# Order of the decay levels and of the constants' loads in a gMLP/HGRN2 trunk kernel

## What is computed

```python
h = _rmsnorm(x, mix_norm[l])
z = h @ w_in[l]
u, v, q, f, i, og, gates = _split_cols(z, IN_SIZES)
a = _gmlp_branch(gelu(u), gelu(v), gm_ln_g[l], gm_ln_b[l], gm_ws[l], gm_bs[l])
b = _hgrn2_branch(q, f, i, og, lower_bounds[l], hg_norm_g[l])
y = sigmoid(gate_a) * (a @ w_br_gm[l]) + sigmoid(gate_b) * (b @ w_br_hg[l])
x = x + y @ w_out[l]
x = x + _conv_ffn(_rmsnorm(x, ffn_norm[l]), w_up[l], conv_w[l], conv_b[l], w_down[l])
# then a last rmsnorm.  Inside _gmlp_branch: w masked to blocks of 64 positions,
mixed = einsum('hij,bnjhd->bnihd', w, layernorm(v)) + bs
# Inside _hgrn2_branch, per head and chunk, G the running sum of log(forget):
A = einsum('bhid,bhijd,bhjd->bhij', q, exp(G_i - G_j) where causal, k)
o = A @ v + (q * exp(G)) @ state
state = exp(G_last) * state + (k * exp(G_last - G))^T @ v
```

## Time and profile before

| | us |
|---|---|
| median of 3 runs (lowest to highest) | 2891.79 (2891.43 to 2895.05) |
| the profiled execution | 2889.99 |
| its span, first to last instruction | 2888.2 |
| around the span | 1.8 |
| TensorE busy | 2858.6 |
| VectorE, ScalarE, GpSimd busy | 1511.7, 724.3, 196.2 |
| mean granted TensorE clock | 0.997 |

### The profile page before, as it was taken

The page is one execution under the profiler, slowest core; times in us unless marked ns, Lnnn a source line. Parts: engine busy times, 40 slices in busy tenths (PEclk is TensorE's granted clock), DMA queues, the critical chain, the costliest instruction groups (busy, mean ns, idle before and its releaser), DMA issues.

```text
span 2888.2 us, 33313 instructions
## 1 busy us (share of the span) xinstructions
PE 2858.6 (99%) x13264; PEld 2380.4 (82%) x13264; DVE 1511.7 (52%) x2879; ACT 724.3 (25%) x986; POOL 196.2 (7%) x87
## 2 busy tenths in 40 slices
PE   8999999999999999999999999999999999999998
PEld 6888888888888888888888888888888888888886
DVE  6876677756266335553335634555333653455521
ACT  5332244434212112221112211222112220122200
POOL 3333410015000000000000000000000000000000
PEclk9999999999999999999999999999999999999999
DMA  8657988889744465556563446555666345555554
GB/s 299 233 187 236 318 288 289 292 303 330 256 146 147 164 227 191 190 194 231 213 222 132 161 170 219 194 189 192 234 216 218 132 146 190 208 198 191 190 211 167
DMA packets 121977, 614.58 MB, mean 213 GB/s; under 512 B 13536, under 2 KB 13792, under 8 KB 74080
## 3 DMA queue, kind: packets, MB, share of 16 engines
q1 hardware_dynamic: 121824, 612.46, 60.2%
HBM read 474.00 MB, written 138.41 MB: 212 GB/s over the span
## 4 chain that ended last, share of the span: by engine, by line
PE 94%; DVE 2%; DMA 1%; issue 1%; POOL 1%; ACT 0%; POOLq 0%; SPq 0%; DVEq 0%; ACTq 0%
PE bank L1008 27%; PE bank L1009 27%; PE bank L1013 27%; PE bank L1075 3%; PE bank L1062 2%; PE bank L1063 2%; PE bank L1064 2%; DMA raw<-w_units 1%; POOL w_both L409 1%; PE bank L1148 1%; PE bank L1177 0%; DMA w_split<-w_both 0%; PE bank L1169 0%; PE bank L1022 0%; PE bank L1019 0%
## 5 line engine op out<-in xcount | busy, mean ns | idle before, releaser
L1008 PE MATMUL bank<-h_hi,w_both 128*128 128x512 f32 x2400 | 944.4, 393 | 0.0
L1009 PE MATMUL bank<-h_lo,w_both 128*128 128x512 f32 x2400 | 934.2, 389 | 0.0
L1013 PE MATMUL bank<-h_hi,w_both 128*128 128x512 f32 x2400 | 593.4, 389 | 0.0
L1008 PEld LDWEIGHTS bank<-h_hi,w_both 128*128 128x128 f32 x2400 | 450.7, 188 | 96.4 <-issue 3.8
L1009 PEld LDWEIGHTS bank<-h_lo,w_both 128*128 128x128 f32 x2400 | 450.6, 188 | 96.1 <-issue 3.8
L1013 PEld LDWEIGHTS bank<-h_hi,w_both 128*128 128x128 f32 x2400 | 450.5, 188 | 93.5
L926 DVE TENSOR_TENSOR z<-bank,rms_inv 128x512 f32<-128x512 f32 x176 | 121.8, 692 | 337.8 <-PE bank L1013 337.4
L1009 PE MATMUL bank<-g_lo,w_both 128*128 128x512 f32 x704 | 273.9, 389 | 0.0
L1008 PE MATMUL bank<-g_hi,w_both 128*128 128x512 f32 x704 | 273.9, 389 | 0.0
L939 DVE SCALAR_TENSOR_TENSOR conv<-z,params,conv 128x512 f32<-128x512 f32 x352 | 263.5, 750 | 7.0 <-DVE halo L929 0.8
L409 POOL TENSOR_TENSOR w_both<-raw,w_both 128x1024 fp32r<-128x1024 f32 x80 | 195.0, 2438 | 533.3 <-ACT w_both L423 493.3
(11 more groups left out here) (220 smaller groups left out, 3139.3 us busy)
## 6 DMA issues: line engine op xcount, KB each, us to landing
w_both<-w_split SPq DMA_DIRECT2D x372, 1024.0 KB, 4.8
w_split<-w_both SPq DMA_DIRECT2D x248, 512.0 KB, 5.6
raw<-w_units SPq DMA_DIRECT2D x124, 512.0 KB, 5.3
x_in<-x_t SPq DMA_DIRECT2D x32, 256.0 KB, 5.4
res<-x_t SPq DMA_DIRECT2D x32, 256.0 KB, 5.1
out<-res SPq DMA_DIRECT2D x32, 256.0 KB, 6.9
masks<-masks_in SPq DMA_DIRECT2D x1, 1152.0 KB, 9.7
gm_w<-gm_wt SPq DMA_DIRECT2D x1, 256.0 KB, 6.3
```

Of the source, the lines that this page charges most:

```text
L1008: pe.matmul(dst, w_hi[slot][:, off + k, :], rhs_hi(k), start=first and k == 0, stop=False)
L1009: pe.matmul(dst, w_hi[slot][:, off + k, :], rhs_lo(k), start=False, stop=False)
L1013: mm = pe.matmul(dst, w_lo[slot][:, off + k, :], rhs_hi(k), start=False, stop=last and k == n - 1)
```

## The change

On SP the three constants are issued behind units 2, 3 and 4 of tile 0, and the masks behind unit 5. GpSimd's part of `gm_w` moves to its turn for unit 8. TensorE's product of `lnb_row` and `gm_w` moves from behind unit 1 to behind unit 7 and from bank 6 to bank 3; TensorE no longer waits for VectorE's addition of `bs_row`, which moves behind the statistics of v in tile 0, and so does the wait for the masks.

In each of the 16 heads VectorE makes keys and totals of all levels first, then the queries of all levels, each still from `qp` of the level before; `og_act` stands between the copy and the product of level 16. TensorE's `flip` waits for the last copied keys; the levels run from 2 up to 64, each behind a wait for its own `qr`; the masked copies follow the same order.

```diff
-    names = ["forget", "floor", "qp1"]
+    names = ["forget", "floor", "qp1", "qr1"]
     for s in LEVELS:
-        names += [f"qr{s}", f"qp{2 * s}", f"kl{2 * s}", f"kr{2 * s}", f"t{2 * s}"]
+        names += [f"kl{2 * s}", f"kr{2 * s}", f"t{2 * s}"]
+    for s in LEVELS:
+        names += ([f"qr{s}"] if s > 1 else []) + [f"qp{2 * s}"]
...
-        for a, b in ((gm_w[:, :, :], gm_wt), (lnb_row[:, :], ln_b.broadcast_to([P, NH * P])),
-                     (bs_row[:, :], gm_bs.broadcast_to([P, NH * P]))):
-            sp.dma_start(a, b).then_inc(consts_in, 16)
-        sp.dma_start(masks[:, :], masks_in).then_inc(masks_here, 16)
...
                 if t == 0:
                     first_tile(u)
+                    if 2 <= u < 5:
+                        sp.dma_start(consts[u - 2][0], consts[u - 2][1]).then_inc(consts_in, 16)
+                    if u == 5:
+                        sp.dma_start(masks[:, :], masks_in).then_inc(masks_here, 16)
...
-            if u == 2:
+            if u == 8:
                 po.wait_ge(consts_in, N_CONST)
-                po.wait_ge(lo_made, 2)
+                po.wait_ge(lo_made, 8)
                 po.memset(gm_w[GM_CHUNK:P, :, 0:GM_CHUNK], 0.0).then_inc(pro_pool, 1)
...
         dve.wait_ge(ident_here, 16)
-        dve.wait_ge(consts_in, N_CONST)
-        dve.wait_ge(pro_pe, 1)
-        dve.tensor_tensor(gm_b[:, :, :], blocks(bank[6][:, :], P), blocks(bs_row[:, :], P), ALU.add).then_inc(pro_dve, 1)
         norm_inv(0)
...
+            if t == 0:
+                dve.wait_ge(consts_in, N_CONST)
+                dve.wait_ge(pro_pe, 1)
+                dve.tensor_tensor(gm_b[:, :, :], blocks(bank[3][:, :], P), blocks(bs_row[:, :], P),
+                                  ALU.add).then_inc(pro_dve, 1)
+                dve.wait_ge(masks_here, 16)
+                dve.wait_ge(pro_dve, 8)
...
+                    dve.tensor_tensor(k2_l, k_l, spread(t_r, s), ALU.mult).then_inc(*head_dve.did(f"kl{2 * s}"))
+                    dve.tensor_copy(k2_r, k_r).then_inc(*head_dve.did(f"kr{2 * s}"))
+                    dve.tensor_tensor(total[2 * s][:, :], t_l, t_r, ALU.mult).then_inc(*head_dve.did(f"t{2 * s}"))
+                for s in LEVELS:
...
+                    then(f"qp{s}")
+                    dve.tensor_copy(blocks(q_right[s][:, :], s), q_r).then_inc(*head_dve.did(f"qr{s}"))
+                    if s == 16:
+                        dve.wait_ge(*head_act.at("sig_og", it))
+                        dve.tensor_tensor(og_act[:, :], sig_og[:, :], bank[1][:, :], ALU.mult).then_inc(evac[1], 1)
+                    then(f"qr{s}")
+                    dve.tensor_tensor(q_r, blocks(q_right[s][:, :], s), spread(t_l, s),
+                                      ALU.mult).then_inc(*head_dve.did(f"qp{2 * s}"))
...
-                pe.wait_ge(*head_dve.at(f"t{P}", it))
+                pe.wait_ge(*head_dve.at(f"kr{P}", it))
                 flip(bank[2], kp[P]).then_inc(*head_pe.did("k_tok"))
-                for a, b in ((64, 32), (16, 8), (4, 2)):
+                for a, b in ((2, 4), (8, 16), (32, 64)):
+                    pe.wait_ge(*head_dve.at(f"qr{a}", it))
                     level(a)
+                    pe.wait_ge(*head_dve.at(f"qr{b}", it))
                     level(b).then_inc(*head_pe.did(f"s{a}_{b}"))
                 from_h(t, U_HEAD + 5, u, 1, used + 2)
-                pe.wait_ge(*head_dve.at("m2", it))
+                pe.wait_ge(*head_dve.at("m64", it))
```

More of the change, by code:

```diff
@@ L239, in build @@
     head_act = Steps(sem("head_act"), ["i_head", "sig_f", "sig_q", "sig_og", "k_tok", "o_sq", "o_rms"])
-    head_pe = Steps(sem("head_pe"), ["s1", "k_tok", "s64_32", "s16_8", "s4_2", "update", "o", "mix", "o_sum"])
-    names = ["forget", "floor", "qp1"]
+    head_pe = Steps(sem("head_pe"), ["s1", "k_tok", "s2_4", "s8_16", "s32_64", "update", "o", "mix", "o_sum"])
+    names = ["forget", "floor", "qp1", "qr1"]
     for s in LEVELS:
-        names += [f"qr{s}", f"qp{2 * s}", f"kl{2 * s}", f"kr{2 * s}", f"t{2 * s}"]
+        names += [f"kl{2 * s}", f"kr{2 * s}", f"t{2 * s}"]
+    for s in LEVELS:
+        names += ([f"qr{s}"] if s > 1 else []) + [f"qp{2 * s}"]
     head_dve = Steps(sem("head_dve"), ["k"] + names + [f"vh{c}" for c in range(NC)]
-                     + ["m1", "m0", "m64", "m32", "m16", "m8", "m4", "m2", "st0", "st1", "st2", "st3", "st4",
+                     + ["m1", "m0", "m2", "m4", "m8", "m16", "m32", "m64", "st0", "st1", "st2", "st3", "st4",
                         "mix", "a", "a_hi", "a_lo", "inv", "unit", "b", "b_hi", "b_lo"])
@@ L361, in _ @@
         sp.dma_start(ident[:, :], ident_in).then_inc(ident_here, 16)
-        for a, b in ((gm_w[:, :, :], gm_wt), (lnb_row[:, :], ln_b.broadcast_to([P, NH * P])),
-                     (bs_row[:, :], gm_bs.broadcast_to([P, NH * P]))):
-            sp.dma_start(a, b).then_inc(consts_in, 16)
-        sp.dma_start(masks[:, :], masks_in).then_inc(masks_here, 16)
+        consts = ((gm_w[:, :, :], gm_wt), (lnb_row[:, :], ln_b.broadcast_to([P, NH * P])),
+                  (bs_row[:, :], gm_bs.broadcast_to([P, NH * P])))
         for t in range(NT):
@@ L716, in _ @@
         dve.wait_ge(pro_pool, 2)
-        dve.wait_ge(masks_here, 16)
-        dve.wait_ge(pro_dve, 8)
+        dve.wait_ge(pro_dve, 7)
         def final_out(turn):
@@ L774, in _ @@
                                   ALU.mult).then_inc(*head_dve.did("qp1"))
+                then("qp1")
+                q_r = halves(qp[:, :], 1)[1]
+                dve.tensor_copy(q_right1.unsqueeze(3), q_r.rearrange("p (n q) s -> p n q s", n=NC)).then_inc(*head_dve.did("qr1"))
                 for s in LEVELS:
-                    then(f"t{s}" if s > 1 else "qp1")
-                    q_l, q_r = halves(qp[:, :], s)
+                    if s > 1:
+                        then(f"t{s}")
                     k_l, k_r = halves(kp[s][:, :], s)
                     k2_l, k2_r = halves(kp[2 * s][:, :], s)
-                    t_l, t_r = halves(total[s][:, :], 1)
-                    t_l, t_r = t_l[:, :, 0], t_r[:, :, 0]
+                    t_l, t_r = (v[:, :, 0] for v in halves(total[s][:, :], 1))
+                    dve.tensor_tensor(k2_l, k_l, spread(t_r, s), ALU.mult).then_inc(*head_dve.did(f"kl{2 * s}"))
+                    dve.tensor_copy(k2_r, k_r).then_inc(*head_dve.did(f"kr{2 * s}"))
+                    dve.tensor_tensor(total[2 * s][:, :], t_l, t_r, ALU.mult).then_inc(*head_dve.did(f"t{2 * s}"))
+                for s in LEVELS:
+                    q_r = halves(qp[:, :], s)[1]
+                    t_l = halves(total[s][:, :], 1)[0][:, :, 0]
                     if s == 1:
-                        dve.tensor_copy(q_right1.unsqueeze(3), q_r.rearrange("p (n q) s -> p n q s", n=NC)).then_inc(*head_dve.did("qr1"))
                         then("qr1")
@@ L786, in _ @@
                                           t_l.rearrange("p (n q) -> p n q", n=NC), ALU.mult).then_inc(*head_dve.did("qp2"))
[L787 to L796, removed]
+                        continue
+                    then(f"qp{s}")
[6 more added lines that the diff above has]
+                                      ALU.mult).then_inc(*head_dve.did(f"qp{2 * s}"))
                 dve.wait_ge(*ln_dve.at("inv", t))
@@ L802, in _ @@
                                       spreads[:, 1, c:c + 1], ALU.subtract, ALU.mult).then_inc(*head_dve.did(f"vh{c}"))
-                for n, (s, made, before) in enumerate(((1, "s1", f"t{P}"), (0, "s1", "m1"), (64, "s64_32", "m0"),
-                                                       (32, "s64_32", "m64"), (16, "s16_8", "m32"),
-                                                       (8, "s16_8", "m16"), (4, "s4_2", "m8"), (2, "s4_2", "m4"))):
+                for n, (s, made, before) in enumerate(((1, "s1", f"vh{NC - 1}"), (0, "s1", "m1"), (2, "s2_4", "m0"),
+                                                       (4, "s2_4", "m2"), (8, "s8_16", "m4"), (16, "s8_16", "m8"),
+                                                       (32, "s32_64", "m16"), (64, "s32_64", "m32"))):
                     dve.wait_ge(*zero_dve.at("scores", t))
@@ L1109, in _ @@
                     for_first_tokens(n, [bank[b] for b in I_BANKS], True)
[L1110 to L1115, removed]
                     if n == 2:
@@ L1124, in _ @@
                     sums_spread(bank[5], r_hi, r_lo, done_dve.at("sum_lo", t - 1), fin_pe)
-            pe.wait_ge(pro_dve, 8)
             if t:
@@ L1133, in _ @@
             if t == 0:
+                pe.wait_ge(pro_pool, 3)
+                for h in range(NH):
+                    mm = pe.matmul(bank[3][:, h * P:(h + 1) * P], lnb_row[:, h * P:(h + 1) * P], gm_w[:, h, :],
+                                   start=True, stop=True)
+                mm.then_inc(pro_pe, 1)
                 pe.wait_ge(*norm_act.at(f"hi{KD - 1}", 0))
```

## The result

| | before | changed |
|---|---|---|
| median, lowest to highest, us | 2894.88, 2891.43 to 2896.08 (5 runs) | 2878.29, 2877.56 to 2878.95 (5 runs) |
| the profiled execution | 2889.99 | 2877.56 |
| its span | 2888.2 | 2875.8 |

The ratio is 0.9946, 95% interval 0.9935 to 0.9956: 0.54% faster. The forecast was 2881.5; the measured median lies 0.7 us under the low end of the range, 2879.0.

A forecast was written before the change was run, and what follows sets the result against it. TensorE, busy 99% of the span, was taken as the bound, leaving idle or low-clock time to win. Start 5.5 plus tile 0's heads 4.8 make 10.3 us: 2891.8 - 10.3 = 2881.5, range 2879.0 to 2886.5.

The forecast's parts named there:

- The start, net 5.5: Tile 0's start: raw 2 lands sooner without constants and masks ahead, unit 4 starts 6.4 us sooner; 5.5 us won net.
- the 0.9 given back: Behind unit 7: the gm_w matmuls taken out of the start run there instead, costing 0.9 us.
- The full-pipe reading at 400 GB/s: Loads at the start: transfers fill the pipe, no latency; 1.97 MB removed ahead of raw 2 saves 4.9 us.
- The heads in tile 0, net 4.8: Tile 0's four heads: the flip's wait goes, less 0.05 us of new wait a head; 4.8 us won net.
- the wait of 1.24 goes, four times: 4.96: TensorE's flip in tile 0's heads: last keys are ready before TensorE comes, saving 4.96 us.
- The upper bound of 5.0: Tile 0's heads: the most the forecast thought could be won there, 5.0 us.
- `qr64` and the last masked copy: Tile 0's heads, what is late next: level 64's queries by 0.7 us in time, the last masked copy a tie.
- Tiles 1 to 3, "nothing won": The 12 heads of tiles 1 to 3: extra 0.7 us on VectorE lies inside 5 us of slack; no gain or loss.
- A: Start: the clock falls all the same, costing 1.7 us and 0 to 1 more of wait; chance 0.12.
- D: Every head: short matmul groups step with VectorE, the clock falls 16 times, 27.2 us, giving 2908.7; chance 0.02.
- B: Tile 0's heads: last masked copy late; 2890.5 us if one more GpSimd run intervenes; chance 0.08 for over a us a head.
- C: Units 3 to 8: moved constants return 4.9 us as late raw or low parts, giving 2886.4; chance 0.05.

The follow-up runs named there:

- masks_front: The changed kernel with the 1152 KB of masks issued at the start again, only the three small constants moved: median 2882.65 us, ratio 0.9962.
- heads: The kernel before with only the change's new order of work in the heads, constants as before: median 2884.5 us, ratio 0.9969.
- flip_qr32: The changed kernel with TensorE's flip waiting for the copied queries of level 32 instead of the last keys: median 2882.77 us, ratio 0.9963.
- flip_qp64: The changed kernel with the flip waiting for qp64, the query product of level 32: median 2887.42 us over 12 runs, ratio 0.9982.
- late_mask: The changed kernel with VectorE's v_head made twice in each head, ahead of the masked copies: median 2884.75 us, ratio 0.9967.
- order: The kernel before with only TensorE's levels and the masked copies reordered, from 2 up to 64: median 2894.3 us, ratio 1.0003.
- consts: The kernel before with only the moves of constants, masks, memset, gm_w matmuls and bs_row addition, heads as before: median 2885.94 us, ratio 0.9980.
- squares: The changed kernel with ScalarE's squares of x 4 and 5 ahead of unit 2's high part in tile 0: median 2877.53 us, ratio 0.9943.
- again: The kernel before, unchanged, run again as a control: median 2894.9 us, ratio 1.0005.
- flip_late: The changed kernel with the flip waiting for the last product of the queries: median 2920.1 us, ratio 1.0090.

## Why the prediction was right, and where it was not

- *The start, net 5.5: right, a little small.* The moved part alone gives 5.2 us on the lowest times and 6.6 on the medians; in its profile the spread comes 6.4 us sooner, and with the 0.9 given back that is the 5.5 of the sum. By its steps, in the changed kernel: landing at 16.2 (15.9 measured), last sum near 26.5 (26.1), a wait of 0.3 (0.7), unit 4 at 33.3 (33.1: 32.63 and 0.45), no fall of the clock (none). The full-pipe reading at 400 GB/s was confirmed by masks_front. In this profile TensorE also began at 6.98 instead of 7.63, but a kernel with the old start did so too (6.97 in heads), so that is scatter. The moved loads cost nothing that shows; the wait at the change of tiles scatters from 0.3 to 2.2 us in all kernels.
- *The heads in tile 0, net 4.8: mechanism right, size too small.* The failed term is "the wait of 1.24 goes, four times: 4.96". An idle time in this view starts at the modelled end of the last matmul, 0.39 us behind its start, while matmuls follow each other at 0.23 (before):

```profile
18.55 0.39 PE L1100 MATMUL bank<-w_both,hx_hi 128*128 128x512 f32 x1
18.77 0.39 PE L1101 MATMUL bank<-w_both,hx_lo 128*128 128x512 f32 x1
```

  So a wait costs 0.16 more than its line says, and the first matmuls behind it take at least 0.05 longer; flip_qr32 and flip_qp64 measured 0.24 or 0.25 for both. With the order of the levels, 0.07, that makes 1.55 a head, and 1.53 was measured. The upper bound of 5.0 took the idle time for all that could be won; 4 x 1.53 and the 0.8 us of tiles 1 to 3 (below) are 6.9, and the 1.9 us above that bound are more than the 0.7 by which the median lies under the range.
- *`qr64` and the last masked copy: right.* GpSimd's run fell where it was put, on the copy of level 64 instead of on the product before it. The tie at the masked copy was exact: 95.77 against 95.83, no wait, and late_mask shows no slack.
- *Tiles 1 to 3, "nothing won": wrong by 0.8 us*, the order of the levels, 12 x 0.07.
- *The clock in the heads: wrong, and the main miss on the medians.* The argument against rivals A and D was that "the four waits of 1.24 left the clock up". It was read in one execution. In about half of the executions of the kernel before (31 of 63 above 2894) they did not: the times are some 5 us higher at a lower mean clock, one profile (order) shows the fall behind such a wait, and with 1.4 us of wait half the runs are high, with 0.95, none of five. The changed kernel loses these with the wait, so its median gains 16.6 us where its profile gains 12.4. I had taken the 1.8 us between the profiled execution and the first median for noise; with 2895.05 among the three runs shown, 3.3 above the next, it was a sign.
- *The rivals.* A, B, C and D did not come true. D's premise, idle time between the groups of levels, did not arise; its price was real for the waits that the kernel already had, and there it was 4.8 us a fall, not the 1.7 that D took.

That the upper kind of the kernel before is lower clock is on record for its runs. That the fall is in a head is shown by one profile of a kernel with the same wait, by the distance, by consts, which has no fall at the start and keeps the two kinds, and by putting the wait back (flip_qp64); no profile of the kernel before itself caught it. Why the same wait lets the clock fall in one execution and not in the next stays open.

## What to carry to other kernels

Look at the single times before using one profile: two kinds of times with a gap mean that the profile shows only one of them. A wait of TensorE of 1.25 us cost here itself, some 0.24 us more, and now and then 5 us by a lower clock, so a small idle time is worth more than its line in the waits. Loads that nobody needs yet belong behind the ones that the first units wait for, by bytes, the largest first.

## What was not expected of the hardware

- The clock fell behind idle times of 1.25 us (order), 1.48 with 0.79 behind it (late_mask) and 2.15 (squares, at the change of tiles: 0.57 in the 4 us behind it), and for very different lengths: 3.4, 6.8, about 10 and 13.7 us.

```profile
728.00:732.00 4.00, 4.00 (x11) 0.57 0.81 328
```

  All the idle times of 2.7 to 3.4 us ahead of the first sums (before, again, heads, order, masks_front) and of 4.4 ahead of the flip (flip_late) came with a fall too, in three profiles up to 1 us before the wait was over. Of the 28 between 1.0 and 1.8 us two did. No fall is seen where the only idle time is one of 0.98, 0.95 or 0.72. Seven of the 28, of 1.0 to 1.8 us, stand at the change of tiles, ahead of matmuls of 512 columns, and none of the seven brought a fall (again):

```profile
740.61 0.50 PE L1062 MATMUL bank<-w_both,h_hi 128*128 128x512 f32 x1 [1.77 <-DMA w_both<-w_split]
```

  Both falls of the 28 came among narrow matmuls, but 2 of 21 and 0 of 7 are too few to say that the narrow ones matter; no run separates them from the wait.

  At the end of every profile, before and changed alike, the clock falls as well, at or behind the waits of 2.3 and 1.3 us that the last rmsnorm puts ahead of TensorE's last matmuls; the falls counted above are those ahead of it.

  The Trainium skill, "TensorE: Matmul & The Clock Gate", section "What's actually happening", has the low level as the default that activity releases; that fits a fall behind a wait. What decides whether the same wait lets the clock fall in one execution and not in the next, no run here shows.
- The order of six groups of matmuls with the same work changes their time by 0.07 us: the group with 64-column keys is dearer directly behind the transposes.
